# Opening a two-block network: norm, attention tables, forget gate and V merged into one stage

## The reference, cut to what matters

```python
h = rmsnorm(x, norm1_g[l])
proj = h @ w_in[l]
(x_rnn, g_rnn, dq, dk, dv, fq, fk, fv, f_logit, gates) = jnp.split(proj, IN_SPLITS, axis=-1)
o_diff = diff_attention(dq..., dk..., dv..., lam, rel_bias)
log_f = jax.nn.log_sigmoid((f_logit + fox_b_f[l]).astype(jnp.float32))
o_fox = forgetting_attention(fq..., fk..., fv..., log_f)
```

## Time and profile before

| | |
|---|---|
| median of 3 runs | 3721.92 us (3719.7 to 3721.95) |
| the profiled execution, its own time | 3721.45 us |
| its span in the trace | 3719.7 us |
| PE busy | 3180.3 us (85%) |
| DVE, ACT, POOL busy | 1413.8, 1127.9, 778.8 us |
| DMA | 179.01 MB, 48 GB/s over the span |

### The profile page before, as it was taken

One profiled execution on the slowest core, in us unless ns is written; L12 is line 12 of the kernel. 1 busy time (PEld: TensorE's weight loads), 2 busy tenths in 40 slices (PEclk: granted clock), 3 DMA queues, 4 the chain that ended last, 5 costly groups with the idle time before them and its releaser, 6 DMA issues. The chain is left out here.

```text
span 3719.7 us, 41404 instructions
## 1 busy us (share of the span) xinstructions
PE 3180.3 (85%) x15075; PEld 2583.6 (69%) x15075; DVE 1413.8 (38%) x2232; ACT 1127.9 (30%) x1538; POOL 778.8 (21%) x511
## 2 busy tenths in 40 slices
PE   5998899899899899799999995556898878997676
PEld 3776777688777687678878884445677767785455
DVE  4155233311155212443343435643133347213754
ACT  3244233321266221422222223113323332232231
POOL 0100110021212121121212210333222222122651
PEclk9999999999999999899999997758999998998888
DMA  2100110022221222311111101223110000211103
GB/s 106 46 26 10 57 33 23 18 60 67 53 51 38 64 71 79 69 45 39 56 39 56 45 28 68 51 15 85 51 40 23 23 23 23 46 46 51 57 29 113
DMA packets 271060, 179.01 MB, mean 48 GB/s; under 512 B 66024, under 2 KB 246376, under 8 KB 270960
## 3 DMA queue, kind: packets, MB, share of 16 engines
q1 hardware_dynamic: 270960, 177.69, 17.2%
HBM read 158.43 MB, written 19.23 MB: 48 GB/s over the span
## 5 line engine op out<-in xcount | busy, mean ns | idle before, releaser
L136 POOL TENSOR_TENSOR w_low<-w_raw,w_high 128x1024 fp32r<-128x1024 f32 (+1 forms) x183 | 419.8, 2294 | 2052.7 <-ACT w_high L129 2047.8
L154 PE MATMUL pu<-act_high,w_high 128*128 128x512 f32 x1104 | 432.7, 392 | 9.7 <-POOLq L108 8.3
L154 PE MATMUL pu<-act_low,w_high 128*128 128x512 f32 x1104 | 431.5, 391 | 0.0
L154 PE MATMUL pu<-act_high,w_low 128*128 128x512 f32 x1104 | 431.4, 391 | 0.0
L129 ACT ACTIVATE w_high<-w_raw 128x1024 fp32r<-128x1024 f32 (+1 forms) x183 | 182.7, 999 | 433.9 <-PE pp L982 94.9
L154 PE MATMUL pg<-act_high,w_high 128*128 128x512 f32 x576 | 227.9, 396 | 54.9 <-POOL w_low L136 29.7
L154 PEld LDWEIGHTS pu<-act_high,w_high 128*128 128x128 f32 x1104 | 208.6, 189 | 54.1 <-POOLq L108 9.1
L154 PEld LDWEIGHTS pu<-act_high,w_low 128*128 128x128 f32 x1104 | 208.4, 189 | 43.9
L154 PEld LDWEIGHTS pu<-act_low,w_high 128*128 128x128 f32 x1104 | 208.6, 189 | 43.5
L154 PE MATMUL pg<-act_low,w_high 128*128 128x512 f32 x576 | 226.4, 393 | 0.0
L154 PE MATMUL pg<-act_high,w_low 128*128 128x512 f32 x576 | 226.2, 393 | 0.0
(11 more groups left out here) (522 smaller groups left out, 6737.0 us busy)
## 6 DMA issues: line engine op xcount, KB each, us to landing
w_raw<-in_w_in SPq DMA_DIRECT2D x110, 512.0 KB, 4.2
w_raw<-in_ffn_up SPq DMA_DIRECT2D x44, 512.0 KB, 3.8
w_raw<-in_w_out SPq DMA_DIRECT2D x24, 512.0 KB, 4.0
v_raw<-in_ffn_down SPq DMA_DIRECT2D x11, 1024.0 KB, 4.9
acum_rows<-acum_rows SPq DMA_DIRECT2D x16, 512.0 KB, 3.7
x<-in_x SPq DMA_DIRECT2D x8, 512.0 KB, 8.4
m_part<-gate SPq DMA_DIRECT2D x8, 512.0 KB, 2.8
w_raw<-in_w_br_rnn SPq DMA_DIRECT2D x8, 512.0 KB, 6.4
```

The lines of the kernel that those rows point to most:

```text
L136: pool.tensor_tensor(self.low[slot][:, 0:nk, :], self.raw[slot][:, 0:nk, :], self.high[slot][:, 0:nk, :].bitcast(F32), ALU.subtract).then_ ...
L154: last = pe.matmul(out[:, h, :] if not halves else out[h], w[slot][:, k, :], x[:, k, cols], start=(n == 0), stop=(n == 3 * nk - 1))
```

## The change

The norm, the tables, the forget gate and V of "diff" become one stage, `stage_open`. The order on each engine is written by hand, block of rows by block of rows. x is no longer kept whole but in a ring of 6 blocks. The four V weight tiles are loaded behind x's second block. PE's order is: line 0, transposes of blocks 0 and 1, V of block 0, transposes of 2 and 3, V of 1, then line 1, transposes of 4, V of 2, line 2, and so on; the forget gate comes before V of blocks 6 and 7. The lines share two PSUM banks (`pL`) with the forget gate, and their last 128 columns are no longer computed (they are overwritten in both versions). `nxt` now brings the first Q and K tiles. `stage_attention` gets `v_ready`: for "diff" it begins with `project(0, 0)` and makes no V; for "fox" it stays as it was.

```diff
-def stage_attention_tables(core, ahead):
+def stage_open(core, ahead):
     NH = 4
+    RING = 6
...
+        turned = psum(core, ctx, "turned", [P, 2, KD, P])
+        pV = [psum(core, ctx, f"pv{s}", [P, HALF]) for s in range(2)]
+        pL = psum(core, ctx, "pl", [P, 2, HALF])
...   # SP
+                block_of_x(0)
+                sp.dma_start(gain[:, :], io["norm1_g"][0].partition_broadcast(P)).then_inc(sem("gain_loaded"), 16)
                 sp.dma_start(edges[:, :], io["bucket_edges"]).then_inc(sem("edges"), 16)
                 sp.dma_start(rel[:, :], io["rel_bias"]).then_inc(sem("rel"), 16)
+                block_of_x(1)
+                for t in range(4):
+                    values(t)
+                for b in range(2, RING):
+                    block_of_x(b)
...
+                W.load(sp, 0, 0, w_in[:, FOX_F_AT:FOX_F_AT + P])
+                for b in range(RING, NB):
+                    block_of_x(b)
                 for h in range(NH):
+                    if h == 1:
+                        sp.wait_ge(sem("wv_low"), 4)
+                        nxt.load(sp, 1)
+                    sp.wait_ge(sem("line"), h + 1)
                     sp.dma_start(core.lines[h], line[:, h % 2, :])...
+                nxt.load(sp, 0)
...   # POOL
+                for t in range(4):
+                    pool.wait_ge(sem("wv_high"), t + 1)
+                    pool.tensor_tensor(wv_low[t][:, :, :], wv_raw[t][:, :, :], wv_high[t][:, :, :].bitcast(F32), ALU.subtract)...
+                W.split_low(pool, 0, 0)
                 nxt.split_low(pool, 1)
                 nxt.split_low(pool, 0)
...   # PE
+                def lines(h):
+                    if h:
+                        pe.wait_ge(sem("line_low"), h)
+                    for j in range(2):
+                        last = pe.matmul(pL[:, j, :], rel_wide[:, h, :], hot[:, j * HALF:(j + 1) * HALF], start=True, stop=True)
+                    last.then_inc(sem("pl"), 1)
...
+                lines(0); turn(0); turn(1); values(0)
+                turn(2); turn(3); values(1)
+                lines(1); turn(4); values(2)
+                lines(2); turn(5); values(3)
+                lines(3); turn(6); values(4)
+                turn(7); values(5)
+                W.multiply(pe, 0, pL, AH, AL)
+                values(6); values(7)
...   # ACT
+                square(0); values_high(0); square(1); values_high(1); high(0)
+                values_high(2); values_high(3); square(2); high(1); square(3); high(2); values_out(0)
+                square(4); high(3); values_out(1)
+                W.split_high(act, 0, 0)
+                square(5); high(4); values_out(2)
                 nxt.split_high(act, 1)
+                square(6); high(5); values_out(3); square(7); high(6); values_out(4); high(7); values_out(5)
+                nxt.split_high(act, 0)
                 (Abs, Exp, Ln of the forget gate)
-                nxt.split_high(act, 0)
+                values_out(6); values_out(7)
...   # DVE, after hot and rel_wide
+                scale(0); make_line(0); scale(1); low(0); scale(2); low(1); scale(3); low(2); low(3)
+                make_line(1); scale(4); low(4)
+                make_line(2); scale(5); low(5)
+                make_line(3); scale(6); low(6); scale(7); low(7)
                 (z, min, sub and scan of the forget gate)
...
-def stage_attention(core, kind, q_at, k_at, v_at, y0, ahead):
+def stage_attention(core, kind, q_at, k_at, v_at, y0, ahead, v_ready=False):
+    T0 = 0 if v_ready else 2
...
-                for t in range(4):
+                for t in () if v_ready else range(4):
                     WV.wait(pe, t % 2, t // 2)
...
-        stage_norm_to_channels(core, x0, io["norm1_g"][0], io["x"][0], ahead=columns(w_in, FOX_F_AT))
-        stage_attention_tables(core, value_tiles(DV))
-        stage_attention(core, "diff", DQ, DK, DV, 0, value_tiles(FV))
+        stage_open(core, columns(w_in, DQ, DK))
+        stage_attention(core, "diff", DQ, DK, DV, 0, value_tiles(FV), v_ready=True)
```

More of the change, by code:

```diff
@@ L173, in views, with load @@
         return [tile_view(self.slots[part][slot], nk, width) for part in ("raw", "high", "low")]
-    def load(self, sp):
+    def load(self, sp, *slots):
         for slot, src in self.tiles:
+            if slots and slot not in slots:
+                continue
             if self.turns[slot]:
@@ L786, in _, with turn, values @@
                           allow_small_or_imprecise_dtypes=True).then_inc(sem("dist"), 1)
+                for t in range(4):
+                    pool.wait_ge(sem("wv_high"), t + 1)
+                    pool.tensor_tensor(wv_low[t][:, :, :], wv_raw[t][:, :, :], wv_high[t][:, :, :].bitcast(F32), ALU.subtract).then_inc(sem("wv_low"), 1)
+                W.split_low(pool, 0, 0)
                 nxt.split_low(pool, 1)
                 nxt.split_low(pool, 0)
+            @block.tensor
+            def _(pe):
+                W.open_pe(pe)
+                def lines(h):
[4 more added lines that the diff above has]
+                    last.then_inc(sem("pl"), 1)
+                def turn(b):
+                    pe.wait_ge(sem("scaled"), b + 1)
+                    if b >= 2:
+                        pe.wait_ge(sem("low"), b - 1)
+                    for k in range(KD):
+                        last = pe.transpose(turned[:, b % 2, k, :], scaled[b % 2][:, k * P:(k + 1) * P], core.ident[:, :])
+                    last.then_inc(sem("turned"), 1)
+                def values(b):
+                    pe.wait_ge(sem("low"), b + 1)
+                    if b >= 2:
+                        pe.wait_ge(sem("v_out"), b - 1)
+                    for kk in range(KD):
+                        if b == 0 and kk % 2 == 0:
+                            pe.wait_ge(sem("wv_low"), kk // 2 + 1)
+                        for i, (a, w) in enumerate(((AH, wv_high), (AL, wv_high), (AH, wv_low))):
+                            last = pe.matmul(pV[b % 2][:, :], a[:, kk, b * P:(b + 1) * P], w[kk // 2][:, kk % 2, :],
+                                             start=(kk == 0 and i == 0), stop=(kk == KD - 1 and i == 2))
+                    last.then_inc(sem("v_psum"), 1)
+                pe.wait_ge(sem("hot"), 1)
+                pe.wait_ge(sem("rel_wide"), 1)
+                lines(0)
+                turn(0)
+                turn(1)
+                values(0)
+                turn(2)
+                turn(3)
+                values(1)
+                lines(1)
+                turn(4)
+                values(2)
+                lines(2)
+                turn(5)
+                values(3)
+                lines(3)
+                turn(6)
+                values(4)
+                turn(7)
+                values(5)
+                pe.wait_ge(sem("line_low"), NH)
+                pe.wait_ge(sem("low"), NB)
+                W.wait(pe, 0, 0)
+                W.multiply(pe, 0, pL, AH, AL)
+                values(6)
+                values(7)
@@ new lines, in _ @@
+                square(0)
+                values_high(0)
+                square(1)
+                values_high(1)
+                high(0)
+                values_high(2)
+                values_high(3)
+                square(2)
+                high(1)
+                square(3)
+                high(2)
+                values_out(0)
+                square(4)
+                high(3)
+                values_out(1)
+                W.split_high(act, 0, 0)
+                square(5)
+                high(4)
@@ L798, in _, with make_line, scale, low @@
                 act.activation(t[:, :], t[:, :], ACT.Ln, bias=1.0).then_inc(sem("ln"), 1)
-                nxt.split_high(act, 0)
[L801 to L813, removed]
+                values_out(6)
+                values_out(7)
             @block.vector
             def _(dve):
+                def make_line(h):
+                    dve.wait_ge(sem("pl"), h + 1)
+                    if h >= 2:
+                        dve.wait_ge(sem(("line_stored", "line_stored1")[h % 2]), 16)
+                    dve.tensor_copy(line[:, h % 2, 0:SEQ], flat2(pL)).then_inc(sem("line_low"), 1)
+                    dve.wait_ge(sem("line_low"), h + 1)
+                    dve.memset(line[:, h % 2, SEQ:LINE], -NEG).then_inc(sem("line"), 1)
+                def scale(b):
+                    dve.wait_ge(sem("root"), b + 1)
+                    dve.reciprocal(stats[:, 2, b:b + 1], stats[:, 1, b:b + 1]).then_inc(sem("rstd"), 1)
+                    dve.wait_ge(sem("rstd"), b + 1)
+                    if b >= 2:
+                        dve.wait_ge(sem("turned"), b - 1)
+                    dve.scalar_tensor_tensor(out=scaled[b % 2][:, :], in0=x[:, b % RING, :], scalar=stats[:, 2, b:b + 1],
+                                             in1=gain[:, :], op0=ALU.mult, op1=ALU.mult).then_inc(sem("scaled"), 1)
+                def low(b):
+                    dve.wait_ge(sem("high"), b + 1)
```

(37 more changed lines are left out.)

93 lines of the change are left out of this document (69 added, 24 removed).

## The result

| | before | changed |
|---|---|---|
| median | 3720.95 us (3719.7 to 3721.95, 4 runs) | 3688.72 us (3687.52 to 3692.26, 4 runs) |
| span of the profiled execution | 3719.7 us | 3685.8 us |

The ratio is 0.9915, 95% interval 0.9898 to 0.9932: 32 us faster, where 26.2 us had been forecast and 3695.3 us predicted, in the range of 3685 to 3703 us.

The account below looks back on a forecast made before the run. Before `project`, V was bound by PE's matmuls, norm and tables/gate by hand-off chains. Q's start moving from 136.7 to 110.5 us saves 26.2 us: 3721.45 us becomes 3695.3 us, range 3685 to 3703 us.

Parts of the forecast that it names:

- V of block 0 starts: First V matmuls in the new stage, after line 0 and the transposes of blocks 0 and 1: at 19.7 us.
- three cycles with a line: PE's three rounds of line, one block's transposes and an earlier block's V: 14.75 us each, 44.2 us in all.
- the pause in each: PE idle after each of lines 1 to 3, waiting for DVE's copy, memset, reciprocal and scaling: 3.3 us.
- gate's end to `c`: Chain from the forget gate's last matmul to the scan's end: 10.8 us instead of 12.8, `c` ready at 107.5 us.
- store and barrier: End of the stage, between `c` being ready and the first Q matmul: 3.0 us.
- Q: Start of the first Q matmul of `project`: 110.5 us instead of 136.7, 26.2 us less.
- the fall of the clock: PE drops to 1.2 GHz in each line cycle: 14.75 us a cycle, against 11.5 us warm throughout.
- the shorter scan: Forget gate's scan no longer beside a POOL subtraction: 2.3 us instead of 4.31, 2.0 us less.
- the time at the low level of a block that starts cold: Dense matmul block starting at 1.2 GHz: 5.0 us at that rate, so 7.8 us for V of one block.
- the rival with a PE at the low level throughout: Small pieces between V's blocks hold PE at 1.2 GHz: Q at 147.0 us, 3731.8 us; 3 in 100.
- The rival of the warm clock: Clock holds through the line cycles: 9.7 us less than the forecast, 3685.6 us; 2 in 10.
- the dearer case: First part or hand-offs cost more, including scalings caught by POOL and PE cold into Q: 3700 to 3713 us; 12 in 100.

Follow-up runs that it names:

- experiment 1: Changed kernel with DVE's scalings of blocks 4, 5 and 6 put ahead of lines 1, 2 and 3: 3672.86 us; once more on another chip, 3678.73 us.
- experiment 2: Changed kernel with 14 extra throwaway matmuls on PE after each of lines 1 to 3, to fill the pause: 3686.72 us.
- experiment 3: Changed kernel with ACT's high part of the next stage's slot 0 back behind the forget gate's Ln, so POOL's subtraction runs beside the scan: 3692.73 us.
- experiment 4: Changed kernel with V of "diff" taken out of `stage_open` and back in the attention stage; norm, tables and gate stay merged: 3719.26 us.
- experiment 5: Changed kernel with V of "diff" back in the attention stage and DVE's scalings of blocks 4 to 6 ahead of lines 1 to 3: 3715.76 us.
- experiments 6 and 7: 6: forget gate one block earlier, on top of experiment 1, 3673.08 us; 7: also edges, rel and block 1's scaling earlier, 3671.24 us, rerun 3672.99 us.

## Why the prediction was right

Its steps against the trace of the changed kernel:

| | forecast | measured |
|---|---|---|
| line 0 starts | 10.3 us | 10.74 |
| V of block 0 starts | 19.7 | 19.34 |
| V of block 1 ends | 35.1 | 33.6 |
| three cycles with a line | 44.2 | 40.5 |
| the pause in each | 3.3 | 3.23, 3.23, 2.92 |
| gate ends | 96.7 | 91.5 |
| gate's end to `c` | 10.8 | 10.8 |
| store and barrier | 3.0 | 3.15 |
| Q | 110.5 | 105.5 |

The mechanism held: the pause, the fall of the clock, V under the gate's chain and the shorter scan were all there. The pause behind the line was read from the two orders; that it is DVE's order alone is shown by experiment 1. That it came to 3.23 us twice, against the 3.3 forecast, is in part luck. Those two scalings met a POOL subtraction that the forecast did not have there:

```profile
35.36 2.35 POOL L136 TENSOR_TENSOR w_low<-w_raw,w_high 128x1024 fp32r<-128x1024 f32 x1 [12.16 <-ACT w_high L129]
...
37.19 1.59 DVE L969 SCALAR_TENSOR_TENSOR scaled<-x_ring,stats,gain 128x1024 f32<-128x1024 f32 x1
```

The third, without one, took 1.28 us, and its pause was 2.92: the hand-offs and the reciprocal cost 0.4 us less than forecast, the subtraction 0.3 more. The fall of the clock in each of the three cycles was taken over from one pause of 2.40 us in "diff", and experiments 1 and 2 show that it hangs on the pause. The scan's 2.0 us are shown by experiment 3.

The term that was mis-sized is the time at the low level of a block that starts cold. I had put it at 5.0 us between two rows of before (4.0 and 6.0). It was 3.1 us in V of block 0 and 3.1, 2.7 and 3.1 us in V of blocks 2, 3 and 4, which makes 7.0 us a block instead of 7.8. It is not a fixed size: the same kernel run again had 1.8, 1.8, 2.3 and 3.5 us, experiment 3 had 4.3 in V of block 0. The transposes held V up for less than the 1.94 us of the sum: V began 1.09 us after them in the first cycle, in which the clock fell only on the way, and 1.61 us after in the others. Line and pause together came to 5.2, 5.2 and 4.9 us instead of 5.0. So the cycles came to 13.3, 13.8 and 13.4 us instead of 14.75. That is 3.7 of the 5.0 us by which Q came earlier than forecast (some 2.5 from the blocks, 1.5 from the transposes, 0.3 lost on line and pause); V of block 0 gave 0.8 more.

Three smaller things in the working are wrong and moved little. The line was put at 3.4 us cold; by columns, 2,048 of the 2,304 that took 4.2 us make 3.7, and 3.75 was measured (1.98 warm, not 1.7). In the norm no engine reaches two thirds of the stretch, DVE and ACT included (63 and 66%). And the sum of the rival with a PE at the low level throughout leaves V of blocks 6 and 7 fast; at 0.427 us a matmul they take 20.5 us behind the gate, more than its chain, and Q would start at least 7 us later than the 147.0 us given.

The rival of the warm clock (3685.6 us) came near the measured median (3688.72), but not for its reason: the clock did fall. Part of that nearness is the scatter behind Q, 2.7 us here and the other way the second time. The rival on the other side, a PE at the low level throughout, had nothing for it; in the first profile each block of V rose within 3.1 us, in the second within 3.5. Of the dearer case one part was real: the scaling of block 2 took 3.35 us beside POOL's subtractions. It cost nothing, as PE was in V of block 0 until 26.3 us. A second part, PE cold into Q after the pause (put at 2.5 us), was absent in the first profile and there in the second, where `project` took 2.8 us longer.

```profile
18.47 4.73 POOL L832 TENSOR_TENSOR wv_low<-wv_raw,wv_high 128x1024 fp32r<-128x1024 f32 x2 [1.89 <-ACT wv_high L905]
...
20.94 3.35 DVE L969 SCALAR_TENSOR_TENSOR scaled<-x_ring,stats,gain 128x1024 f32<-128x1024 f32 x1
```

What I did not say in the prediction is where the gain sits. The text reads as if the norm's and the tables' chains overlap; experiment 4 shows that in this order they don't, and that the stage would be worth 2.9 us without V in it (8.6 with the scalings first, experiment 5).

## What to carry to other kernels

Merging two chains of small pieces gave little here, since they meet in the same queues; laying a block of dense matmuls into them gave much of that block's length: 28.4 of V's 47.8 us as first written (133.83 to 105.47 us), 37.4 with the scalings first (128.09 to 90.70 us). When orders are written by hand, ask of each engine's queue what stands ahead of the piece that PE needs next: one line moved three times was worth nearly half of this change. And read such edits at a fixed point of the trace (here Q's start), since the time of the whole scatters by some 8 us behind it. But profile the same kernel twice as well: Q's start itself moved by 1.9 us between two executions of the changed kernel, and `project` took 22.0 us in one and 24.8 us in the other.

## What the runs showed of the hardware

Lines of 32 rows in plain fp32 took 3.75 us at the low level and 1.98 us at the high one, and held the high level when there was no pause beside them (experiment 1). The same pause can end either way. The 3.06 or 3.07 us before Q came with a fall of the clock in both profiles of experiment 1, in experiment 2 and in the second profile of the changed kernel, and with none in its first; the 1.85 us came with none in experiments 6 and 7 and with one when 7 was run again.

POOL's subtraction also held up a DVE instruction with one input tensor in SBUF: the minimum `c<-z` took 1.68 us at 94.02 us, beside a subtraction from 92.77 to 95.17 (it ended 0.53 us behind it), and 0.62 us in experiment 3, where POOL was idle. The Trainium skill ("SBUF — State Buffer", section "SBUF: two separate sides") names DVE instructions with two inputs in SBUF and those in a 2-port mode as the ones that exclude GpSimd's. The scalings that met a subtraction fit it (1.4 to 3.5 us instead of 1.28, as in the earlier trace rows and experiment 5); whether the minimum runs in such a mode no run here shows.
